# Decoder trunk on one core: weight sums beside the first three feed-forward out-projections, and the last residual loaded in four pieces

## The chip, the cores and the metric

One core of one Trainium2 chip runs the whole program. The metric is the device time of one execution in microseconds (us); lower is better. Before the change it is 2209.56 us, the median of 3 runs (2207.72 to 2211.31).

## The reference, cut to what matters

```python
D_MODEL = 1024; SEQ = 512; DEPTH = 2; D_FF = 2816

def _swiglu(x, w_in, w_out):
    gate, up = jnp.split(x @ w_in, 2, axis=-1)
    return (jax.nn.silu(gate) * up) @ w_out

for i in range(DEPTH):
    ng = norm_gains[i]
    x = x + 0.5 * _rmsnorm(_swiglu(_rmsnorm(x, ng[0]), ffn1_w_in[i], ffn1_w_out[i]), ng[1])
    h = _rmsnorm(x, ng[2])
    m = _hgrn2(h, ...) if i == 0 else _gated_deltanet(h, ...)
    x = x + _rmsnorm(m, ng[3])
    x = x + 0.5 * _rmsnorm(_swiglu(_rmsnorm(x, ng[4]), ffn2_w_in[i], ffn2_w_out[i]), ng[5])
```

All in float32, 512 tokens of 1024 features. The change touches no formula; it concerns the four feed-forward sub-layers, above all the last line of the second layer, `ffn2_w_out[1]`, and the last addition to `x`.

## The kernel before, in words

**Six stages**, numbered by `s`: feed-forward (0), HGRN2 (1), feed-forward (2 and 3), DeltaNet (4), feed-forward (5). `ffn_no` numbers the feed-forward stages 0 to 3. A float32 product is made of three TensorE passes over operands split in a high and a low part (high by high, high by low, low by high). Weights come as *units* of 128 x 1024 (512 KB) or, in the out-projections, 128 x 768 and 128 x 640. Each unit goes through a ring of four places: SP loads it into `raw`, ScalarE copies it to `w_hi` (L898, L972, in the last out-projection L1147 in `out_high`), VectorE subtracts and writes `w_lo` (L1679, L1798, L2013 in `out_low`), TensorE uses it. SP loads unit n when VectorE has split unit n - 4; ScalarE copies unit n when TensorE has used unit n - 4.

**A feed-forward stage** has an in-projection of some 230 us (six pairs of columns done plainly, L2830, the rest with seven products in place of eight, L2909) and then the out-projection, 8 tiles of 22 blocks of 128 rows each. In stages 0, 2 and 3 the tiles are ordinary ones: ScalarE squares each tile from PSUM into one of the two halves of `sq` (L1230), POOL adds the squares of tiles 0 to 6 up in `acc` (`total` in `sum8`, L2637 for the first and L2640 for the others), and TensorE reads `acc` in the middle of the last tile (L2820, `sum_outputs`). ScalarE's square of tile c waits for the sum of tile c - 2.

**The last out-projection** (stage 5, `out_products`) works by token tile, with seven products p = 0 to 6 of half-size matrices in place of eight. Each product takes 11 half units (128 x 512) of weights, so there are 77 half units, in 39 units n = 0 to 38. Products 0, 1 and 4 take their weights from `last_out` as they are. Products 2, 3, 5 and 6 take sums and differences of its four quarters. Those are not computed by an engine: POOL's queue makes them beforehand with accumulating DMA transfers in DRAM, into `w_sums`, 11 row tiles k of 128 x 4 x 512. Each k takes five transfers: 768 KB and 256 KB of plain copies, an add of 768 KB, an add of 768 KB, an add of 256 KB, where each add waits on `sums_added` until what went before it has landed. `weight_sums` does k = 0 to 5 in stage 2 and k = 6 to 10 in stage 3, each time before that stage's `sum8`, one k after the other. SP waits for all of them once, before unit n = 11.

**The order of the work in the last out-projection** is written out by hand. VectorE's loop calls `out_low(n)` for n = 4 to 38 and does other work after some of them: `part_low("s1")` after n = 15, `part_low("s4")` after n = 16 (L2007, the low parts of activation quarters), two `joined` after n = 20 (L2038), `part_low("s3")` after n = 21, `part_low("a22")` after n = 22. ScalarE's loop calls `out_high(n)`, and after n = 20 makes two high parts (`part_high`, L1140). SP's loop loads unit n (L812, two transfers of 256 KB), and after n = 20 it loads the residual by token, `x_tok` (2 MB, one transfer, L817), and the last gain row broadcast to 128 partitions into `out_gain` (512 KB, L818). `out_gain` lies in the memory of `y`, which the SwiGLU products of the last quad still read (`last_rows`, L1867, semaphore value `last_early`). VectorE waits for both transfers (`tok_loaded`) after its last `out_low`; then come the scalings L2047 and the final additions L2050.

Of the kernel before, what the change touches and what calls it, by code (L numbers as in the profile page):

```python
# [17 lines left out]
P = 128  # L18
TOK = 512
D = 1024  # L20
KD = D // P
# [17 lines left out]
KH = KF // 2  # L39
# [13 lines left out]
def trunk(nc, A, out, kinds=("ffn", "hg", "ffn", "ffn", "gd", "ffn")):  # L53
# [4 lines left out]
    ALU = mybir.AluOpType  # L58
# [3 lines left out]
    first_unit, total = [], 0  # L62
# [3 lines left out]
    ffn_no = {s: n for n, s in enumerate(s for s, k in enumerate(kinds) if k == "ffn")}  # L66
    LAST = len(kinds)

    ctx = ExitStack()
    with ctx:  # L70
# [140 lines left out]
        unit_used = sem("unit_used")  # L211
# [11 lines left out]
        x_rows_stored = sem("x_rows_stored")  # L223
        tok_loaded = sem("tok_loaded")
# [10 lines left out]
        act_ready = sem("act_ready")  # L235
# [4 lines left out]
        dve_rows = sem("dve_rows")  # L240
# [32 lines left out]
        sums_added = sem("sums_added")  # L273
# [217 lines left out]
        def last_early(s, t):  # L491
            return up_early(s, QUADS - 1, t) + 2
# [10 lines left out]
        def part_ready(name):  # L503
            return KF * (len(ffn_no) - 1) + PARTS.index(name) + 1
# [17 lines left out]
        def mixed(n):  # L522
            return DVE_ROWS * len(ffn_no) + n
# [200 lines left out]
        def _(sp):  # L724
# [15 lines left out]
            def ffn(s):  # L740
                u0 = first_unit[s]
                w_in = A["ffn_in"]
                w_out = A["ffn_out"]
                row0 = ffn_no[s] * 2 * KF

                def weights(row):
                    return w_in[row:row + 1, :, :].rearrange("a p n -> (a p) n")

                def rows_of(q):
                    return row0 + 2 * PLAIN + 8 * q  # L750

                def gate_quarter(q, a):
                    sp.wait_ge(joint_made, joint(s, q - 1, "rest", a))
                    sp.wait_ge(lo_split, unit_of(s, q - 1, 6) + a + 1 + SKEW)
                    sp.dma_start(gate_place(s, q, a), weights(rows_of(q) + a)).then_inc(quarter_loaded[0][a], 16)

                def lower_gate_quarter(q, a):
                    if q == 1:
                        sp.wait_ge(unit_used, u0 + 2 * PLAIN)
                    else:  # L760
                        sp.wait_ge(lo_split, unit_of(s, q - 2, 3) + a + 1 + SKEW)
                    sp.dma_start(lower_gate_place(s, q, a), weights(rows_of(q) + 2 + a)).then_inc(quarter_loaded[1][a], 16)

                def up_quarter(q, a):
                    if q == 0:
                        sp.wait_ge(unit_used, u0 + 2 * PLAIN)
                    else:
                        sp.wait_ge(lo_split, unit_of(s, q - 1, 7) + a + 1 + SKEW)
                    sp.dma_start(up_place(a), weights(rows_of(q) + 4 + a)).then_inc(quarter_loaded[2][a], 16)

                def lower_up_quarter(q, a):
                    if q == 0:
                        sp.wait_ge(unit_used, u0 + 2 * PLAIN)
                    else:
                        sp.wait_ge(lo_split, unit_of(s, q - 1, 4) + a + 1 + SKEW)
                    sp.dma_start(lower_up_place(s, q, a), weights(rows_of(q) + 6 + a)).then_inc(quarter_loaded[3][a], 16)

                for n in range(0 if s else RING, 2 * PLAIN):
                    load((u0 + n, 0), weights(row0 + n))
                if s == LAST - 1:  # L780
                    for c in range(KD):
                        sp.wait_ge(turned, c + 1)
                        for a in range(P // SUB):
                            src = x_turned[a * SUB:(a + 1) * SUB, :, :].rearrange("i c (b j) -> i c b j", j=SUB)
                            dst = x_rows.rearrange("(b i) (c a j) -> a i c b j", i=SUB, a=P // SUB, j=SUB)[a]
                            sp.dma_start(dst[:, c], src[:, c]).then_inc(x_rows_stored, 16)
                for n in range(2 * PLAIN, N_PLAIN):
                    load((u0 + n, 0), weights(row0 + n))
                for q in range(QUADS):
                    if q:  # L790
                        for a in range(2):
                            gate_quarter(q, a)
                        for a in range(2):
                            lower_gate_quarter(q, a)
                    for a in range(2):
                        up_quarter(q, a)
                        if q == 0:
                            lower_up_quarter(q, a)
                    if q:
                        for a in range(2):  # L800
                            lower_up_quarter(q, a)
                if s < LAST - 1:
                    out_loads(s, w_out, ffn_no[s] * KD)
                    return
                v0 = u0 + IN_UNITS["ffn"]
                for n in range(OUT_PARTS):
                    sp.wait_ge(lo_split, v0 + n - RING + 1 + SKEW)
                    if n == KH:
                        sp.wait_ge(sums_added, SUMS)
                    for a in range(half_weights(n) // TOK):  # L810
                        cols = slice(a * TOK, (a + 1) * TOK)
                        sp.dma_start(raw[:, (v0 + n) % RING, cols], half_source(2 * n + a)).then_inc(raw_loaded[(v0 + n) % RING], 16)  # L812
                    if n == 20:
                        sp.wait_ge(act_ready, part_ready("s1"))
                        sp.wait_ge(dve_rows, mixed(6))
                        sp.wait_ge(x_rows_stored, 16 * 4 * KD)
                        sp.dma_start(x_tok[:], x_rows.rearrange("(t p) d -> p t d", p=P)).then_inc(tok_loaded, 16)  # L817
                        sp.dma_start(out_gain, A["last_gain"].to_broadcast([P, D])).then_inc(tok_loaded, 16)  # L818

            def out_loads(s, w_out, row0):  # L820
                cuts = CUTS[kinds[s]]
# [852 lines left out]
        def _(dve):  # L1674
# [341 lines left out]
            def out_products(s):  # L2016
# [40 lines left out]
                for n in range(4, OUT_PARTS):  # L2057
# [38 lines left out]
                    elif n == 36:  # L2096
# [2 lines left out]
                            joined(5, i, right(2 + i), right(2 + i))  # L2099
                        for i in range(2):  # L2100
                            joined(5, i, left(2 + i), left(2 + i))
                dve.wait_ge(tok_loaded, 2 * 16)
                for t in range(2):
                    dve.wait_ge(tok_root, 3 + t)
                    gained(left(t), left(t), 1.0, 0)
# [525 lines left out]
        def _(pool):  # L2631
            def total(q, c, par, first=False):

                pool.wait_ge(sq_done, SQUARES * (q // 2) + KD * (q % 2) + c + 1)
                if first:
                    wait(pool, sum_ready, pre_sums(q // 2) if q else 0)
                    nc.gpsimd.tensor_copy(acc[:], sq[:, par, :]).then_inc(acc_done, 1)  # L2637
                else:
                    pool.wait_ge(acc_done, POOLED * q + c)
                    nc.gpsimd.tensor_tensor(acc[:], acc[:], sq[:, par, :], ALU.add).then_inc(acc_done, 1)  # L2640
# [122 lines left out]
                    if n == 3:  # L2763
                        substitute(range(23, SUB - 1))

            def weight_sums(ks):
                w = A["last_out"]

                def quarter(r, c, k, copies):
                    src = w[(r * KH + k) * P:(r * KH + k + 1) * P, c * TOK:(c + 1) * TOK]  # L2770
                    return src.unsqueeze(1).to_broadcast([P, copies, TOK])

                for k in ks:
                    n = 5 * 16 * k
                    sums = w_sums[k]
                    nc.gpsimd.dma_start(sums[:, 0:3, :], quarter(0, 0, k, 3)).then_inc(sums_added, 16)
                    nc.gpsimd.dma_start(sums[:, 3:4, :], quarter(0, 1, k, 1)).then_inc(sums_added, 16)
                    pool.wait_ge(sums_added, n + 32)
                    nc.gpsimd.dma_start(sums[:, 0:3, :], quarter(0, 1, k, 3), accum_op=ALU.add).then_inc(sums_added, 16)
                    pool.wait_ge(sums_added, n + 48)  # L2780
                    nc.gpsimd.dma_start(sums[:, 1:4, :], quarter(1, 1, k, 3), accum_op=ALU.add).then_inc(sums_added, 16)
                    pool.wait_ge(sums_added, n + 64)
                    nc.gpsimd.dma_start(sums[:, 2:3, :], quarter(1, 0, k, 1), accum_op=ALU.add).then_inc(sums_added, 16)
                    pool.wait_ge(sums_added, n + 80)

            nc.gpsimd.memset(ident[:], 0.0).then_inc(ident_made, 1)
            nc.gpsimd.memset(upper[:], 1.0).then_inc(ident_made, 1)
# [5 lines left out]
            for s, kind in enumerate(kinds):  # L2793
                if s == 0:
                    sum8(0)
                if kind != "ffn":
                    {"hg": hgrn2, "gd": deltanet}[kind](s)
                elif ffn_no[s] in (1, 2):
                    weight_sums(range(6) if ffn_no[s] == 1 else range(6, KH))
                if s < LAST - 1:  # L2800
                    sum8(2 * s + 1)

# [835 lines left out]
```

## Time and profile before

| | |
|---|---|
| median of 3 runs | 2209.56 us (2207.72 to 2211.31) |
| the profiled execution, its own time | 2208.14 us |
| its span | 2206.4 us |
| TensorE matmul busy | 2176.8 us, 99% |
| VectorE, ScalarE, POOL busy | 1598.8, 1164.8, 256.5 us |
| granted TensorE clock | full, but for the last us |
| DMA | 248.96 MB, of it 31.72 MB on POOL's software queue |

The profiled execution's own time is 1.7 us above its span and 1.4 us under the median. Matmul ends are modelled, so the idle time of weight loads (PEld) is the better measure of a short stop of TensorE: one load follows the other in 0.227 us when nothing waits.

### The profile page before, as it was taken

Reading aid. Unit: us, or ns where it says so; the run is one execution under the profiler, and the core shown is the slowest. Engines: PE = TensorE matmul, PEld = TensorE weight load, DVE = VectorE, ACT = ScalarE, POOL = GpSimd, SP = SyncE. Lnnn points to the kernel's source line nnn. Section 1 sums busy time; section 2 is a strip of 40 time slices with the busy share of each in tenths; the row PEclk is TensorE's granted clock in tenths of the full one; section 3 lists DMA queues with packets and bytes.
Section 4 is the critical chain, followed back from the end, with each engine's and each line's share of the span. In section 5 each row is a group of like instructions: output and inputs, shape, how many; then the busy total and the mean of one; then the engine's idle time right before and its main releaser. Section 6 shows DMA issues by size and latency. Waiting matters only on the chain.

```text
span 2206.4 us, 30954 instructions
## 1 busy us (share of the span) xinstructions
PE 2176.8 (99%) x11576; PEld 1804.4 (82%) x11576; DVE 1598.8 (72%) x2044; ACT 1164.8 (53%) x1648; POOL 256.5 (12%) x262
## 2 busy tenths in 40 slices
PE   9999999999999999999999999999999999999998
PEld 8888888888788888888788887777888888788876
DVE  6999536777568987348989337877766644898987
ACT  5455434655554455345445335577666744444563
POOL 2000000100121110011100000022822100000000
PEclk9999999999999999999999999999999999999999
DMA  5322332222267872367762332321212232433264
GB/s 173 125 86 81 108 98 87 87 76 78 69 155 182 225 160 86 97 151 167 192 180 66 99 102 67 101 77 55 83 56 68 68 95 78 116 134 124 86 219 157
DMA packets 106239, 248.96 MB, mean 113 GB/s; under 512 B 26848, under 2 KB 31072, under 8 KB 106112
## 3 DMA queue, kind: packets, MB, share of 16 engines
q1 hardware_dynamic: 92032, 215.24, 30.8%
q0 software_dynamic: 13552, 31.72, 8.1%
q8 instruction: 84, 1.38, 0.3%
q14 instruction: 43, 0.35, 0.1%
q10 hardware_dynamic: 528, 0.26, 0.0%
HBM read 242.93 MB, written 35.98 MB: 126 GB/s over the span
## 4 chain that ended last, share of the span: by engine, by line
PE 84%; DVE 10%; ACT 3%; DMA 1%; issue 1%; SPq 0%; DVEq 0%; ACTq 0%
PE bank L2830 38%; PE bank L2909 24%; PE bank L3275 9%; PE bank L3031 3%; DVE w_lo L1679 2%; PE bank L2983 1%; DVE h_lo L1684 1%; DVE w_lo L1798 1%; DMA raw_last<-in_ffn_in 1%; ACT h_hi L910 1%; ACT w_hi L898 1%; PE bank L3437 1%; DVE resid L1714 1%; PE bank L3416 1%; PE bank L3444 1%
## 5 line engine op out<-in xcount | busy, mean ns | idle before, releaser
L1679 DVE TENSOR_TENSOR w_lo<-raw,w_hi 128x1024 fp32r<-128x1024 f32 x261 | 321.1, 1242 | 334.5 <-ACT w_hi L898 334.1
L2909 PE MATMUL bank<-w_hi,factor 128*128 128x512 f32 x1792 | 553.8, 390 | 3.9 <-DVE w_lo L1798 3.7
L2909 PEld LDWEIGHTS bank<-w_hi,factor 128*128 128x128 f32 x1792 | 335.0, 188 | 75.2 <-issue 4.9
L898 ACT ACTIVATE w_hi<-raw 128x1024 fp32r<-128x1024 f32 x261 | 271.5, 1054 | 214.6 <-PE bank L2830 193.6
L2909 PE MATMUL bank<-w_lo,factor 128*128 128x512 f32 x896 | 349.1, 390 | 0.0
L2830 PE MATMUL bank<-h_hi,w_hi 128*128 128x512 f32 (+1 forms) x775 | 295.2, 381 | 5.7 <-DVE h_lo L1684 2.7
L2830 PE MATMUL bank<-h_hi,w_lo 128*128 128x512 f32 (+1 forms) x775 | 284.8, 367 | 0.0
L2830 PE MATMUL bank<-h_lo,w_hi 128*128 128x512 f32 (+1 forms) x748 | 274.6, 367 | 0.0
L2830 PE MATMUL bank<-act_late,w_hi 128*128 128x512 f32 (+1 forms) x648 | 200.7, 367 | 0.0
L2909 PEld LDWEIGHTS bank<-w_lo,factor 128*128 128x128 f32 x896 | 168.2, 188 | 35.2
L2830 PEld LDWEIGHTS bank<-h_hi,w_hi 128*128 128x128 f32 x775 | 146.2, 189 | 37.1 <-issue 6.5
L2830 PE MATMUL bank<-act_lo,w_hi 128*128 128x512 f32 (+1 forms) x540 | 169.6, 366 | 0.0
L2830 PEld LDWEIGHTS bank<-h_hi,w_lo 128*128 128x128 f32 x775 | 146.1, 189 | 24.5
L2830 PEld LDWEIGHTS bank<-h_lo,w_hi 128*128 128x128 f32 x748 | 141.2, 189 | 24.4 <-issue 2.6
L2830 PE MATMUL bank<-act_late,w_lo 128*128 128x512 f32 (+1 forms) x432 | 158.1, 366 | 0.0
L3275 PE MATMUL bank<-h_hi,w_hi 128*128 128x512 f32 x360 | 149.7, 416 | 1.2 <-DVE conv_in L2266 0.7
L3275 PE MATMUL bank<-h_hi,w_lo 128*128 128x512 f32 x360 | 148.4, 412 | 0.0
L3275 PE MATMUL bank<-h_lo,w_hi 128*128 128x512 f32 x360 | 147.3, 409 | 0.0
L2830 PEld LDWEIGHTS bank<-act_late,w_hi 128*128 128x128 f32 x648 | 118.8, 189 | 19.6
L972 ACT ACTIVATE w_hi<-raw_more 128x1024 fp32r<-128x1024 f32 x80 | 84.6, 1061 | 80.4 <-DVE raw_more L1814 32.7
L972 ACT ACTIVATE w_hi<-raw 128x1024 fp32r<-128x1024 f32 x72 | 76.4, 1061 | 70.3 <-PE bank L2909 56.8
L2830 PEld LDWEIGHTS bank<-act_lo,w_hi 128*128 128x128 f32 x540 | 99.5, 189 | 16.6
(388 smaller groups left out, 3959.0 us busy)
## 6 DMA issues: line engine op xcount, KB each, us to landing
raw<-in_ffn_in SPq DMA_DIRECT2D x84, 512.0 KB, 4.7
w_sums<-in_last_out POOLq DMA_DIRECT2D x33, 768.0 KB, 8.5
raw<-in_gd_in SPq DMA_DIRECT2D x49, 512.0 KB, 3.7
raw_more<-in_ffn_in SPq DMA_DIRECT2D x48, 512.0 KB, 4.8
raw_last<-in_ffn_in SPq DMA_DIRECT2D x40, 512.0 KB, 6.1
raw<-in_ffn_out SPq DMA_DIRECT2D x48, 384.0 KB, 3.1
raw<-in_hg_in SPq DMA_DIRECT2D x32, 512.0 KB, 3.7
raw<-in_ffn_out SPq DMA_DIRECT2D x48, 320.0 KB, 2.9
```

Source lines behind the costliest of these rows:

```text
L898: nc.scalar.activation(w_hi[:, u[0] % RING, :], raw[:, u[0] % RING, :], ACT.Copy).then_inc(hi_split, 1)
L910: nc.scalar.activation(h_hi[:, c, half(h)], x[:, c, half(h)], ACT.Copy, scale=pre_gain(s, c)).then_inc(h_hi_ready, 1)
L972: nc.scalar.activation(w_hi[:, u % RING, :], place, ACT.Copy).then_inc(hi_split, 1)
L1679: nc.vector.tensor_tensor(w_lo[:, r, :], raw[:, r, :], w_hi[:, r, :].bitcast(f32), ALU.subtract).then_inc(lo_split, 1)
L1684: nc.vector.scalar_tensor_tensor(out=h_lo[:, c, half(h)], in0=x[:, c, half(h)], scalar=pre_gain(s, c), in1=h_hi[:, c, half(h)].bitcast(f32 ...
L1714: nc.vector.tensor_tensor(x[:, c, half(h)], x[:, c, half(h)], y[:, i % 2, half(h)], ALU.add).then_inc(x_ready, 1)
L1798: TT(w_lo[:, u % RING, :], place, w_hi[:, u % RING, :].bitcast(f32), ALU.subtract).then_inc(lo_split, 1)
L2830: ins = nc.tensor.matmul(dst[:, half(h)], w, moving[ml][:, k, :][:, half(h)], start=first and n == 0 and (wl, ml) == (0, 0), stop=last and ...
L2909: ins = nc.tensor.matmul(bank[dst[t]][:], factor[:, 2 * i + ml, at:at + P], (w_hi, w_lo)[wl][:, u % RING, b * TOK:(b + 1) * TOK], start=st ...
L2983: ins = nc.tensor.transpose(dst[:, t * P:(t + 1) * P], rows[:, f * P:(f + 1) * P], ident[:])
L3031: ins = nc.tensor.matmul(product_bank(p, i)[:], operands[p][ml][:, k, i * P:(i + 1) * P], (w_hi, w_lo)[wl][:, u % RING, cols], start=k == ...
L3275: ins = MM(bank[unit_bank(n)][:], (w_hi, w_lo)[wl][:, (u0 + n) % RING, k * P:(k + 1) * P], (h_hi, h_lo)[ml][:, k, :], start=x == 0, stop=x ...
```

## The change

POOL's five transfers per k are no longer done k by k. In the out-projection of each of stages 0, 2 and 3, two groups of tiles k, `(0, 1), (2, 3)`, then `(4, 5), (6, 7)`, then `(8, 9), (10,)`, go through their steps between the seven `total` calls, the k's of a group together. The wait for a step's transfers stands after the next `total` and before the next step's transfers. `out_gain` is loaded after unit n = 5 instead of n = 20, behind a wait for unit 0's use and for `last_rows`. `x_tok` is loaded in four transfers of one token tile (512 KB) after units 20, 23, 26 and 29.

```diff
@@ sync, ffn, last out-projection
-                    if n == 20:
-                        sp.wait_ge(act_ready, part_ready("s1"))
-                        sp.wait_ge(dve_rows, mixed(6))
-                        sp.wait_ge(x_rows_stored, 16 * 4 * KD)
-                        sp.dma_start(x_tok[:], x_rows.rearrange("(t p) d -> p t d", p=P)).then_inc(tok_loaded, 16)
+                    if n == 5:
+                        sp.wait_ge(unit_used, v0 + 1)
+                        sp.wait_ge(dve_rows, last_early(s, 1))
                         sp.dma_start(out_gain, A["last_gain"].to_broadcast([P, D])).then_inc(tok_loaded, 16)
+                    if n in (20, 23, 26, 29):
+                        t = (n - 20) // 3
+                        if t == 0:
+                            sp.wait_ge(act_ready, part_ready("s1"))
+                            sp.wait_ge(dve_rows, mixed(6))
+                            sp.wait_ge(x_rows_stored, 16 * 4 * KD)
+                        sp.dma_start(x_tok[:, t, :], x_rows[t * P:(t + 1) * P, :]).then_inc(tok_loaded, 16)
@@ vector, out_products
-                dve.wait_ge(tok_loaded, 2 * 16)
+                dve.wait_ge(tok_loaded, 5 * 16)
@@ gpsimd
-            def weight_sums(ks):
...
+            SUM_TILES = (((0, 1), (2, 3)), ((4, 5), (6, 7)), ((8, 9), (10,)))
...
+            def begin_sums(ks):
                 for k in ks:
...
+                    nc.gpsimd.dma_start(w_sums[k][:, 0:3, :], quarter(0, 0, k, 3)).then_inc(sums_added, 16)
+                    nc.gpsimd.dma_start(w_sums[k][:, 3:4, :], quarter(0, 1, k, 1)).then_inc(sums_added, 16)
+
+            def add_to_sums(ks, added, a, b, r, c):
+                pool.wait_ge(sums_added, 16 * added)
+                for k in ks:
+                    nc.gpsimd.dma_start(w_sums[k][:, a:b, :], quarter(r, c, k, b - a), accum_op=ALU.add).then_inc(sums_added, 16)
+
+            def sum8_beside_sums(q, first, second):
+                n = 5 * first[0]
+                m = 5 * second[0]
+                f, g = len(first), len(second)
+                total(q, 0, 0, True)
+                begin_sums(first)
+                total(q, 1, 1)
+                add_to_sums(first, n + 2 * f, 0, 3, 0, 1)
+                total(q, 2, 0)
+                add_to_sums(first, n + 3 * f, 1, 4, 1, 1)
+                total(q, 3, 1)
+                add_to_sums(first, n + 4 * f, 2, 3, 1, 0)
+                begin_sums(second)
+                total(q, 4, 0)
+                add_to_sums(second, m + 2 * g, 0, 3, 0, 1)
+                total(q, 5, 1)
+                add_to_sums(second, m + 3 * g, 1, 4, 1, 1)
+                total(q, 6, 0)
+                add_to_sums(second, m + 4 * g, 2, 3, 1, 0)
@@ gpsimd, loop over the stages
-                elif ffn_no[s] in (1, 2):
-                    weight_sums(range(6) if ffn_no[s] == 1 else range(6, KH))
-                if s < LAST - 1:
+                if kind == "ffn" and s < LAST - 1:
+                    sum8_beside_sums(2 * s + 1, *SUM_TILES[ffn_no[s]])
+                elif s < LAST - 1:
                     sum8(2 * s + 1)
```

## Rows read from the trace of the kernel before

**Rows 1.** The page, busy time of each engine in the whole span.

```profile
PE 2176.8 (99%) x11576; PEld 1804.4 (82%) x11576; DVE 1598.8 (72%) x2044; ACT 1164.8 (53%) x1648; POOL 256.5 (12%) x262
```

**Rows 2.** Waits of weight loads, 2120 to 2165 us: us in total, times, longest.

```profile
PEld bank L3031 <- DVE w_lo L2013: 4.7, 4, 1.5
```

**Rows 3.** SP's queue from 2130 us: start, us, what was issued.

```profile
2133.03 0.37 SPq L817 DMA_DIRECT2D x_tok<-x_rows  x1
2136.26 0.82 SPq L812 DMA_DIRECT2D raw<-w_sums  x2
```

**Rows 4.** DMA, 2120 to 2165 us: count, KB each, median us to landing.

```profile
x_tok<-x_rows SPq DMA_DIRECT2D x1, 2048.0 KB, 8.8
y<-in_last_gain SPq DMA_DIRECT2D x1, 512.0 KB, 10.8
```

**Rows 5.** ScalarE from 2133 us: start, us, what ran, idle before, releaser.

```profile
2133.40 1.06 ACT L1147 ACTIVATE w_hi<-raw 128x1024 fp32r<-128x1024 f32 x1 [1.65 <-PE bank L3031]
...
2137.63 4.99 ACT L1140 ACTIVATE act_parts<-y_all 128x2816 fp32r<-128x2816 f32 x2
2145.72 1.06 ACT L1147 ACTIVATE w_hi<-raw 128x1024 fp32r<-128x1024 f32 x1 [3.11 <-DMA raw<-w_sums]
```

**Rows 6.** VectorE from 2135 us.

```profile
2135.01 4.62 DVE L2013 TENSOR_TENSOR w_lo<-raw,w_hi 128x1024 fp32r<-128x1024 f32 x4
...
2146.82 1.23 DVE L2013 TENSOR_TENSOR w_lo<-raw,w_hi 128x1024 fp32r<-128x1024 f32 x1 [5.98 <-ACT w_hi L1147]
2147.96 3.08 DVE L2007 TENSOR_TENSOR act_lo<-y_all,act_parts 128x2816 fp32r<-128x2816 f32 x1
2150.96 1.22 DVE L2013 TENSOR_TENSOR w_lo<-raw,w_hi 128x1024 fp32r<-128x1024 f32 x1
2152.09 3.08 DVE L2007 TENSOR_TENSOR act_lo<-y_all,act_parts 128x2816 fp32r<-128x2816 f32 x1
```

**Rows 7.** TensorE's weight loads at the first of those four stops.

```profile
2136.29 0.30 PEld L3031 LDWEIGHTS bank<-w_hi,act_parts 128*128 128x128 f32 x2 [0.63 <-DVE w_lo L2013]
```

**Rows 8.** Waits of weight loads in stage 3's in-projection, 980 to 1225 us.

```profile
PEld bank L2909 <- issue: 1.7, 2, 1.1
PEld bank L2909 <- DVE w_lo L1798: 1.4, 1, 1.4
```

**Rows 9.** The same waits in stage 2's in-projection, 630 to 870 us.

```profile
PEld bank L2909 <- issue: 1.1, 1, 1.1
...
PEld bank L2909 <- DVE w_lo L1798: 0.2, 1, 0.2
```

**Rows 10.** VectorE shortly before stage 3's longest stop.

```profile
1056.94 1.23 DVE L1802 TENSOR_TENSOR raw<-raw_more,raw 128x1024 f32<-128x1024 f32 x1 [1.18 <-DMA raw_more<-in_ffn_in]
```

**Rows 11.** VectorE at the start of the last out-projection.

```profile
2090.18 1.28 DVE L1867 TENSOR_TENSOR y_first<-y_first,y 128x512 f32<-128x512 f32 x2
...
2104.12 3.49 DVE L2013 TENSOR_TENSOR w_lo<-raw,w_hi 128x1024 fp32r<-128x1024 f32 x3
```

**Rows 12.** ScalarE's copy of unit 6 there.

```profile
2098.42 1.04 ACT L1147 ACTIVATE w_hi<-raw 128x1024 fp32r<-128x1024 f32 x1
```

**Rows 13.** POOL in stage 0's out-projection: first and last of its seven sums.

```profile
250.80 0.61 POOL L2637 COPY acc<-sq 128x512 f32<-128x512 f32 x1 [231.64 <-ACT sq L1230]
...
340.49 1.30 POOL L2640 TENSOR_TENSOR acc<-acc,sq 128x512 f32<-128x512 f32 x1 [13.50 <-ACT sq L1230]
```

**Rows 14.** TensorE's first reading of POOL's sum in stage 0.

```profile
350.41 0.60 PE L2820 MATMUL bank<-acc,ones 128*128 128x256 f32 x2
```

**Rows 15.** POOL's queue, the third step of the weight sums of k = 0.

```profile
641.41 1.26 POOL L2781 DMA_DIRECT2D w_sums<-in_last_out  x1 [10.62 <-DMA w_sums<-in_last_out]
```

**Rows 16.** DMA, 620 to 1140 us: packets, MB, share of 16 engines; one issue.

```profile
q0 software_dynamic: 13552, 31.72, 34.4%
...
raw_last<-in_ffn_in SPq DMA_DIRECT2D x18, 512.0 KB, 7.0
```

**Rows 17.** Stage 2's out-projection: five engines' busy time, clock, DMA share, GB/s.

```profile
880.00:970.00 90.00, 90.00 (x431) 75.94 (x431) 29.42 (x24) 31.29 (x36) 9.07 (x8) 1.00 0.39 109
```

More of the change, by code:

```diff
@@ L2764, in deltanet @@
                         substitute(range(23, SUB - 1))
-            def weight_sums(ks):
[L2767 to L2771, printed above, removed]
-                for k in ks:
[L2774 to L2784, printed above, removed]
@@ new lines, in _, with quarter @@
+            SUM_TILES = (((0, 1), (2, 3)), ((4, 5), (6, 7)), ((8, 9), (10,)))
+            def quarter(r, c, k, copies):
+                src = A["last_out"][(r * KH + k) * P:(r * KH + k + 1) * P, c * TOK:(c + 1) * TOK]
+                return src.unsqueeze(1).to_broadcast([P, copies, TOK])
+            def begin_sums(ks):
+                for k in ks:
+                    nc.gpsimd.dma_start(w_sums[k][:, 0:3, :], quarter(0, 0, k, 3)).then_inc(sums_added, 16)
+                    nc.gpsimd.dma_start(w_sums[k][:, 3:4, :], quarter(0, 1, k, 1)).then_inc(sums_added, 16)
```

## The prediction

> **What bounds the kernel now.** I read the page's busy times first: TensorE's matmuls are busy for 99% of the span [rows 1], so only what stops TensorE can cost or give time. Next I read the waits of its weight loads, stretch by stretch. Two stops have to do with the transfers that the change moves.
>
> The larger is in the last out-projection: 4.7 us in four stops, all for VectorE's `out_low` [rows 2]. Such an idle time holds 0.04 us of ordinary gap (a load of 0.19 us every 0.227 us), and after a stop two loads take 0.30 us where they otherwise take 0.42, so 0.12 us is caught up [rows 7]. Net loss: 4.7 - 4 x 0.16 = 4.1 us. The queue tells why. At 2133.03 SP issues 2 MB of residual and then 512 KB of gain, and only at 2136.26 unit 21 [rows 3]. The 2.5 MB land 8.8 and 10.8 us after issue [rows 4]. ScalarE ends its two high parts at 2137.63 + 4.99 = 2142.6 and then waits 3.1 us for unit 21 [rows 5], VectorE waits 5.98 us for ScalarE, and behind unit 21 it must do two low parts of 3.08 us, with unit 22 between them [rows 6]. So the lateness of unit 21 hits units 21, 22 and 23.
>
> The smaller is in stage 3's in-projection: 1.7 + 1.4 = 3.1 us of idle loads [rows 8] against 1.1 + 0.2 = 1.3 us at the same place of stage 2 [rows 9]. VectorE had waited 1.18 us for a weight unit there [rows 10], while the weight sums ran. Less 0.12 us caught up at its stop, and some 0.1 for the shorter one, about 1.6 us is lost. Stage 2 ran with such sums too and lost nothing more: it is a matter of phase.
>
> **The residual in four pieces, the gain early.** I work the queue out anew. Before unit 21 stand 512 KB in place of 2.5 MB. At the rate of the 2.5 MB (issued at 2133.0, the last landed at 2133.4 + 10.8 = 2144.2: 0.23 MB/us [rows 3, 4]) that is 2.3 us, so unit 21 lands by about 2141, before ScalarE is free at 2142.6. ScalarE then copies it to 2143.6. VectorE splits it from 2143.6 and goes on at its own pace (1.14 us to the next operation after a split, 3.0 after a low part [rows 6]): s3 from 2144.8, unit 22 from 2147.8 to 2149.0, a22 from 2148.9, unit 23 from 2151.9 to 2153.1. TensorE's times: a unit takes 12 x 0.227 = 2.72 us (ScalarE's 1.06 + 1.65 beside it [rows 5]); unit 17 starts at 2136.29 [rows 7], so 21 at 2147.2, 22 at 2149.9, 23 at 2152.6. Unit 21 is ready 2.4 us early, 22 by 0.9, 23 is 0.5 late. The first stop, 0.63 us, stays: unit 17 is the first of four splits that start at 2135.01 [rows 6], behind the low parts of s1 and s4, before any residual was asked for. Left are 0.63 - 0.16 = 0.5 and 0.5 - 0.1 = 0.4 us. **Gain: 4.1 - 0.9 = 3.2 us.** If TensorE had still to wait for the pieces, the gain would be less; its ends are 0 (unit 21 as late as now) and 4.1 (no stop left). I take 3.2, which follows from rows at 1 us from the place.
>
> The later pieces go after units 23, 26 and 29. Each puts 512 KB before the next unit, in a stretch where three units (1.5 MB) are used in 8.2 us. 2 MB in 8.2 us is 0.24 MB/us, about what the 2.5 MB and its followers got. The last is issued when unit 25 is split, near 2156, and is wanted after unit 38, some 30 us later. I cost them at nothing; the cover is the ring, which asks for a unit four units (10.9 us) before TensorE needs its place.
>
> The trace says nothing against small transfers there. The Trainium skill, DMA: Bandwidth & Descriptors, Measured, says the opposite of this edit: transfers should be 1 MiB or more, and each has a fixed cost of about 2 us. By that, three more transfers cost an estimated 6 us of DMA time, which would lie in the queue, not on TensorE, while units land in time. No row here shows 512 KB pieces of the residual.
>
> The gain row: SP now stops after unit 5 until `last_rows` ends at 2090.18 + 1.28 = 2091.5 [rows 11]. Queued behind it is unit 6, which now is asked for when unit 2 is split, some 2 us before that, and from then on with 512 KB ahead of it. ScalarE copies unit 6 at 2098.42 [rows 12], VectorE splits it at 2104.12 [rows 11]. Bounds: with the 7.0 us of a unit beside other traffic [rows 16] it lands near 2099 and is copied by 2100; with the 10.8 us of the loaded queue [rows 4] it lands at 2102.8 and is copied by 2103.9, still before VectorE's turn. Both ends are zero for TensorE. On the other side the change takes 512 KB out of the busy stretch (in the sum above).
>
> **The weight sums.** Removed from the in-projections: all their traffic. The extra stop of stage 3 goes, **1.6 us** (ends 0 and 1.8). Added to the out-projections of stages 0, 2 and 3: POOL's issues (22 + 33 as before, about 1 us each) and waits. Queued behind the waits is the next `total`; ScalarE waits for it a whole tile later, and TensorE for the last one. The seven sums are 14.96 us apart, from 250.80 to 340.49 [rows 13], and TensorE reads the result at 350.41 [rows 14]. The last `total` stands behind five waits (begin, two adds, the mixed step, an add). From 251.4 on, the fifth may end at 350.4 - 1.3 (sum) - 2.5 (two issues) = 346.6: **19.0 us per step** is the point from which TensorE waits. What is a step with two k's? One add of 768 KB took 1.3 + 10.6 = 11.9 us with its issue [rows 15]; two are 13.2 us if they overlap and 23.8 if not. POOL's queue used 34.4% of 520 us for 11 k's, 16.3 us of all sixteen engines per k [rows 16], so two k's need 32.5 us over four steps, 8.1 us each, more in the adds (about 11); the weights of the out-projection take 39% of the engines [rows 17]. 11 / 0.7 + 1.3 gives about 17 us; the mixed step 19, the first 16. Sum 16 + 3 x 17 + 19 = 86: TensorE's sum is ready some 9 us before its time. So zero, with ends at zero and at 5 x 23.8 - 95 = 24 us in each of two stages, some 12 in the third with its smaller second group.
>
> Weight units beside them: a load is asked for four units (15 us) before ScalarE's copy, and under the sums' traffic a 512 KB unit landed in 7.0 us [rows 16]. TensorE has three units more. Zero.
>
> **Sum.** 3.2 + 1.6 = 4.8 us off the profiled execution: 2208.1 to 2203.3. That execution is 1.4 us under the median of the three, so the median is predicted at 2209.6 - 4.8 = **2204.8 us**. About 0.2%, 4.4 us, is what a measurement of this kernel can tell from no change, so the forecast stands just beyond it.
>
> **Rivals.**
> 1. *Both stops go* (forecast), range 2203 to 2206. For: the queue's order and the times above. Chance 0.50.
> 2. *Only a part is real*: the stop of stage 3 is a matter of phase and may be missing in other executions or return elsewhere, or the pieces (a small transfer's fixed cost) keep unit 21 late by 1 to 2 us more. Gain 3.2 alone, or 1.6 + 1.5: 2206.4. Chance 0.28. Against: unit 21 has 1.5 us to spare before ScalarE.
> 3. *More goes*: no stop is left in the last out-projection, and stage 3 gives its upper end: 4.1 + 1.8 and up to 1 us elsewhere: 2203.2. Chance 0.12.
> 4. *POOL's last sum comes late* (slower). Place: the wait before the last `total`, then L2820. It decides above 19.0 us per step and outweighs the gain above 19.5. At 20 us a step it is 5 us late in stages 0 and 2: 2209.6 + 10 - 4.8 = 2214.8. For: the ends reach to 23.8. Against: the engine time. Chance 0.10, half of it beyond 0.2% slower. In a sentence that the sum does not need: the Trainium skill, DMA: Bandwidth & Descriptors, Arbitration, says each engine takes turns between queue rows packet by packet; POOL's adds would then get at least half of each engine beside SP's loads, 11 / 0.5 + 1.3 = 23 us a step at worst, and only while SP's row is never empty, which the 39% speaks against.
>
> **The numbers.** Faster by over 0.2%: 0.38 of case 1, 0.11 of case 3, a little of 2: 0.50. Slower: 0.06. Same: 0.44. The range 2202.0 to 2208.8 holds cases 1 to 3 and the spread of the medians; case 4 is left out.
>
> **What would show it.** Right: idle of weight loads at L3031 falls from 4.7 to about 1.2 us in two stops (units 17 and 23), unit 21 is not waited for by ScalarE; stage 3's in-projection idles like stage 2's; POOL's L2640 in stage 0 still starts near every 15 us and L2820 is never waited for. Wrong: a wait of L2820 for POOL, DMA waits of L1147 after 2142 us, or a stop of unit 6 near 2106.

## The result, and the profile after

The changed kernel is slower: 2230.81 us, the median of 4 runs (2230.01 to 2235.4), against 2210.43 us before (4 runs). The ratio is 1.0099, 95% interval 1.0084 to 1.0114, a loss of about 20 us. I had forecast 2204.8 us and a gain. The place where it was lost stood among the rivals as the fourth, with a chance of 0.10 and a price that was too small.

The profiled execution of the changed kernel is its slowest, 2235.4 us, with a span of 2233.6; the one before had 2206.4, so 27.2 us are to be explained there. (The change adds lines: L1140 is now L1145, L1147 is L1152, L1230 is L1235, L1679 is L1684, L2013 is L2018, L2640 is L2645, L2776 and L2777 are L2779 and L2780, all adds of the weight sums are L2785, L2820 is L2841, L2909 is L2930, L3031 is L3052.)

The waits of TensorE's weight loads in the whole span (us in total, times, longest):

```profile
PEld bank L2841 <- POOL acc L2645: 28.2, 2, 15.0
```

This line did not exist before. TensorE, in the middle of the last tile of an out-projection, twice waited for POOL's last sum of squares. POOL's queue in stage 0's out-projection shows the way there, from the first sum to the last transfer (compare [rows 13, 14]):

```profile
250.96 0.61 POOL L2642 COPY acc<-sq 128x512 f32<-128x512 f32 x1 [231.60 <-ACT sq L1235]
...
265.94 1.29 POOL L2645 TENSOR_TENSOR acc<-acc,sq 128x512 f32<-128x512 f32 x1 [11.64 <-ACT sq L1235]
267.19 1.32 POOL L2785 DMA_DIRECT2D w_sums<-in_last_out  x1
277.57 1.26 POOL L2785 DMA_DIRECT2D w_sums<-in_last_out  x1 [9.06 <-issue]
...
286.80 1.25 POOL L2785 DMA_DIRECT2D w_sums<-in_last_out  x1 [4.60 <-DMA w_sums<-in_last_out]
297.25 1.24 POOL L2785 DMA_DIRECT2D w_sums<-in_last_out  x1 [9.20 <-issue]
298.04 1.77 POOL L2645 TENSOR_TENSOR acc<-acc,sq 128x512 f32<-128x512 f32 x1
307.86 1.70 POOL L2785 DMA_DIRECT2D w_sums<-in_last_out  x2 [8.05 <-DMA w_sums<-in_last_out]
...
330.93 1.29 POOL L2785 DMA_DIRECT2D w_sums<-in_last_out  x1 [1.39 <-DMA w_sums<-in_last_out]
342.44 1.24 POOL L2785 DMA_DIRECT2D w_sums<-in_last_out  x1 [10.21 <-issue]
...
352.41 1.25 POOL L2785 DMA_DIRECT2D w_sums<-in_last_out  x1 [7.42 <-DMA w_sums<-in_last_out]
361.16 1.22 POOL L2785 DMA_DIRECT2D w_sums<-in_last_out  x1 [7.50 <-issue]
361.95 1.72 POOL L2645 TENSOR_TENSOR acc<-acc,sq 128x512 f32<-128x512 f32 x1
370.09 1.69 POOL L2785 DMA_DIRECT2D w_sums<-in_last_out  x2 [6.42 <-DMA w_sums<-in_last_out]
```

Two things are to be seen. The steps are longer than I took them: from one wait's end to the next 19.6, 21.1, 23.1 and 21.5 us. And the second transfer of a pair of adds is not issued after the first: POOL's queue stands still for 7.5 to 10.2 us with no semaphore to wait for ("issue"), and only then issues it. I call that a held issue. So the last sum, which stands behind a pair, starts at 361.95 in place of 340.49, and TensorE reads it at 363.7 instead of 350.4.

What the stop does to TensorE's clock, in the columns of [rows 17] (five engines' busy time, clock, DMA share, GB/s):

```profile
352.00:354.00 2.00, 0.00 (x0) 0.00 (x0) 0.00 (x0) 0.00 (x0) 1.25 (x1) 1.00 0.01 4
354.00:356.00 2.00, 0.00 (x0) 0.00 (x0) 0.00 (x0) 0.00 (x0) 0.00 (x0) 0.59 0.84 76
356.00:364.00 8.00, 0.28 (x1) 0.28 (x2) 0.00 (x0) 0.00 (x0) 2.51 (x2) 0.50 0.59 96
364.00:366.00 2.00, 2.00 (x6) 1.64 (x7) 0.00 (x0) 0.17 (x1) 0.00 (x0) 0.50 1.11 125
366.00:368.00 2.00, 2.00 (x12) 2.00 (x11) 0.91 (x2) 0.73 (x2) 0.00 (x0) 0.50 1.01 150
368.00:370.00 2.00, 2.00 (x18) 2.00 (x18) 0.61 (x1) 1.46 (x2) 0.00 (x0) 1.00 0.30 53
```

TensorE's last matmul before the stop ended at 350.7. The granted clock stays full until about 354.4 and is then at the lower of its two levels (1.2 GHz) until 368, 4.3 us after TensorE went on: 6 and 12 matmuls in 2 us, then 18. Stage 2's stop looks much the same, with 3.4 us at the lower level after it. The account of the profiled execution: 28.2 us of stops, less the 4.8 us that I had worked out for the two gains below, leaves 23.4; the span grew by 27.2. The 3.8 that remain are what 4.3 + 3.4 us at half clock cost, by this estimate.

The two gains that I had worked out are there. The waits of weight loads, first in the last out-projection (2130 to 2200 us), then in a stretch with stage 3's in-projection (980 to 1260 us):

```profile
PEld bank L3052 <- DVE w_lo L2018: 1.6, 2, 1.0
...
PEld bank L2930 <- issue: 1.1, 1, 1.1
```

That is 1.6 us in two stops where 4.7 in four stood [rows 2], and stage 3 idles as stage 2 did [rows 8, 9]. ScalarE no longer waits for unit 21 (compare [rows 5]):

```profile
2168.08 5.00 ACT L1145 ACTIVATE act_parts<-y_all 128x2816 fp32r<-128x2816 f32 x2
2172.98 1.04 ACT L1152 ACTIVATE w_hi<-raw 128x1024 fp32r<-128x1024 f32 x1
```

Behind unit 21, ScalarE does wait for the loads of units 22, 23 and 24, by 0.44, 0.29 and 1.48 us. I had called such waits a sign of being wrong. They cost nothing here: VectorE, which they could hold up, works without idle from 2174.05 us to past its split of unit 23 at 2182.33.

### The profile page after: what moved, and what is told of

Its sections match the earlier page's. It is cut to its first block, busy times and chain, and to the rows that moved or that the text cites. A ratio compares the mean times of both kernels' runs of the same rounds, so it can differ in the third digit from the quotient of the medians.

```text
span 2233.6 us, 30931 instructions
## 1 busy us (share of the span) xinstructions
PE 2179.4 (98%) x11576; PEld 1806.8 (81%) x11576; DVE 1599.9 (72%) x2044; ACT 1166.4 (52%) x1648; POOL 257.1 (12%) x262
## 4 chain that ended last, share of the span: by engine, by line
PE 75%; DVE 10%; issue 6%; DMA 3%; ACT 3%; POOL 1%; SPq 0%; DVEq 0%; ACTq 0%; POOLq 0%
PE bank L2851 30%; PE bank L2930 23%; PE bank L3296 9%; DMA w_sums<-in_last_out 3%; PE bank L3052 3%; DVE w_lo L1684 2%; PE bank L3004 1%; DVE h_lo L1689 1%; DVE w_lo L1803 1%; ACT h_hi L915 1%; POOL w_sums L2785 1%; ACT w_hi L903 1%; DVE resid L1719 1%; PE bank L3458 1%; PE bank L3437 1%
## 5 line engine op out<-in xcount | busy, mean ns | idle before, releaser
L1684 DVE TENSOR_TENSOR w_lo<-raw,w_hi 128x1024 fp32r<-128x1024 f32 x261 | 323.0, 1250 | 335.3 <-ACT w_hi L903 335.0
L2930 PE MATMUL bank<-w_hi,factor 128*128 128x512 f32 x1792 | 553.2, 390 | 2.8 <-DVE w_lo L1803 2.8
L2930 PEld LDWEIGHTS bank<-w_hi,factor 128*128 128x128 f32 x1792 | 335.0, 188 | 73.1 <-issue 4.3
L2930 PE MATMUL bank<-w_lo,factor 128*128 128x512 f32 x896 | 348.8, 389 | 0.0
L2930 PEld LDWEIGHTS bank<-w_lo,factor 128*128 128x128 f32 x896 | 168.2, 188 | 35.3
```

Of the source, the lines that this page charges most:

```text
L1684: nc.vector.tensor_tensor(w_lo[:, r, :], raw[:, r, :], w_hi[:, r, :].bitcast(f32), ALU.subtract).then_inc(lo_split, 1)
L2930: ins = nc.tensor.matmul(bank[dst[t]][:], factor[:, 2 * i + ml, at:at + P], (w_hi, w_lo)[wl][:, u % RING, b * TOK:(b + 1) * TOK], start=st ...
```

## The experiments

All were timed beside the kernel before: it took 2210.78 us (25 runs) beside e1 to e4, and 2210.24 us (25 runs) beside e5 to e8. Each ratio is to the kernel before, with its 95% interval.

**e1, SP's part alone.** The kernel before, with the diff of the SP queue and VectorE's wait; POOL as before.

> The kernel before with SP's part of the change alone (gain row after unit 5, residual in four pieces). Theory (the residual's part works as worked out, all of the loss comes from POOL): 3.2 us faster than before, idle of weight loads at the last out-projection 4.7 -> about 1.6 us in two stops, as in the changed kernel. Rival (part of the loss is here): same as before or slower.

2206.02 us; ratio 0.9982 (0.9973 to 0.9990), 4 us faster. The idle for `out_low` is 1.5 us in two stops. So this part does what was worked out, and none of the loss is here.

**e2, POOL's part alone.** The kernel before, with `sum8_beside_sums` in place of `weight_sums`; SP as before.

> The kernel before with POOL's part alone (weight sums in stages beside the out-projections). Theory (TensorE waits in stages 0 and 2 for POOL's last sum of squares): 20.4 + 3.2 = about 24 us slower than before, two waits of 12 to 15 us for POOL at the reading of the sum, none in stage 3, stage 3's in-projection idling like stage 2's. Rival (the two parts work on each other): anything under 18 us.

2235.89 us; ratio 1.0114 (1.0094 to 1.0134), 25 us slower. The waits of its weight loads (without SP's lines, L2841 is L2836 here, L3052 is L3047):

```profile
PEld bank L2836 <- POOL acc L2640: 26.5, 2, 13.6
PEld bank L3047 <- DVE w_lo L2013: 4.8, 4, 1.5
```

Two waits for POOL, and the four stops of before. The two parts add up: 25 less 4 is the 20 of the whole change, within the intervals.

**e3, more room for descriptors.**

```diff
-    nc = bacc.Bacc("TRN2", target_bir_lowering=False, num_devices=1, dynamic_dma_scratch_size=2048)
+    nc = bacc.Bacc("TRN2", target_bir_lowering=False, num_devices=1, dynamic_dma_scratch_size=3584)
```

2204.05 us; ratio 0.9971 (0.9962 to 0.9980). With this number alone the loss of 20 us becomes a gain of 6: it is worth some 26 us, and I had expected 20 to 25. POOL's queue from the first pair of adds on:

```profile
268.54 2.59 POOL L2785 DMA_DIRECT2D w_sums<-in_last_out  x2
282.26 1.30 POOL L2645 TENSOR_TENSOR acc<-acc,sq 128x512 f32<-128x512 f32 x1 [11.12 <-ACT sq L1235]
286.31 1.24 POOL L2785 DMA_DIRECT2D w_sums<-in_last_out  x1 [2.76 <-DMA w_sums<-in_last_out]
295.12 1.24 POOL L2785 DMA_DIRECT2D w_sums<-in_last_out  x1 [7.57 <-issue]
...
348.26 2.50 POOL L2785 DMA_DIRECT2D w_sums<-in_last_out  x2 [8.68 <-DMA w_sums<-in_last_out]
349.82 2.26 POOL L2645 TENSOR_TENSOR acc<-acc,sq 128x512 f32<-128x512 f32 x1
```

The first and the last pair are issued at once (2.59 and 2.50 us for two), pairs between are still held: POOL's idle put down to issue falls from 135 to 65 us, not under 50 as I expected. The first pair's step takes 17.8 us (268.54 to 286.31), and 19.6 in the changed kernel, where its second issue is held. The rival, that the engines' rate is all, falls. Counted from the first transfer, the last sum is ready 13.0 us earlier than in the changed kernel: 7.5 us because the last pair is issued at once, 5.5 us because the five steps are shorter (95.4 us in place of 100.9). It is just in time; TensorE waited 0.25 us for it.

**e4, the last total first.**

```diff
                 add_to_sums(second, m + 2 * g, 0, 3, 0, 1)
                 total(q, 5, 1)
+                total(q, 6, 0)
                 add_to_sums(second, m + 3 * g, 1, 4, 1, 1)
-                total(q, 6, 0)
                 add_to_sums(second, m + 4 * g, 2, 3, 1, 0)
```

> The changed kernel with the seventh total moved before the wait and the two adds that stood ahead of it; all transfers are as before. Theory (only that total's place behind the step costs time): it runs near 345 us of the span in stage 0, 5 us before TensorE reads the sum; no wait for POOL at either place, 4 to 5 us faster than the kernel before. Rival (what comes later on POOL's queue, the constants of stage 1 behind the last steps, or the transfers that run into the next stage, hold TensorE too): 0 to 10 us slower than before, with new waits after 357 us.

2203.35 us; ratio 0.9972 (0.9961 to 0.9982), 6 us faster than before and 27 faster than the changed kernel. The descriptors' room is the small one and the transfers wait as before; only one addition of 1.3 us stands elsewhere. POOL, and TensorE's reading of the sum:

```profile
342.04 1.24 POOL L2785 DMA_DIRECT2D w_sums<-in_last_out  x1 [11.05 <-issue]
342.83 3.21 POOL L2645 TENSOR_TENSOR acc<-acc,sq 128x512 f32<-128x512 f32 x2
351.90 1.25 POOL L2785 DMA_DIRECT2D w_sums<-in_last_out  x1 [5.86 <-DMA w_sums<-in_last_out]
```

```profile
350.21 0.31 PEld L2841 LDWEIGHTS bank<-acc,ones 128*128 128x128 f32 x2
```

The sum is ready at 346.0, 4 us before it is read. With e2 this settles the cause: the seventh `total` behind that pair of adds. The gain of 6 us is what the change is worth without it; I had worked out 4.8.

**e5, e3 and e4 together.**

> The changed kernel with the last total first (as in e4) and dynamic_dma_scratch_size 3584 (as in e3). Theory (each alone frees TensorE wholly, what they cure is one and the same wait): no further gain, within 1 us of e4, 2203 to 2204. Rival (POOL's late constants of stage 1, at 373 us in e4, still cost something): 1 to 3 us under e4.

2204.13 us; ratio 0.9975 (0.9964 to 0.9985). No further gain: both cure the same wait. POOL's constants of stage 1 come at 362 us here and at 373 in e4, so their lateness cost e4 nothing that these times show.

**e8, room between the two.** As e3, with 2816.

> The changed kernel with dynamic_dma_scratch_size 2816, between 2048 and 3584. Theory (room for descriptors): between the two, issue waits of POOL between 65 and 135 us, at least one of TensorE's two waits shorter than 13 us, time 2204 to 2225. Rival (3584 passes a threshold that 2816 does not): as the changed kernel, 2230.

2207.03 us; ratio 0.9988 (0.9979 to 0.9997). POOL's idle for issue is 53 us, below the 65 that I gave as the lower end and less than at 3584, yet TensorE still waits, 3.7 us in two waits. POOL's queue, and the first of the two waits:

```profile
268.06 2.60 POOL L2785 DMA_DIRECT2D w_sums<-in_last_out  x2
...
286.55 2.52 POOL L2785 DMA_DIRECT2D w_sums<-in_last_out  x2 [3.47 <-DMA w_sums<-in_last_out]
...
303.42 1.69 POOL L2785 DMA_DIRECT2D w_sums<-in_last_out  x2 [5.38 <-DMA w_sums<-in_last_out]
...
324.60 2.54 POOL L2785 DMA_DIRECT2D w_sums<-in_last_out  x2 [4.76 <-DMA w_sums<-in_last_out]
...
341.70 1.24 POOL L2785 DMA_DIRECT2D w_sums<-in_last_out  x1 [13.24 <-DMA w_sums<-in_last_out]
350.77 1.24 POOL L2785 DMA_DIRECT2D w_sums<-in_last_out  x1 [7.83 <-issue]
```

```profile
353.35 0.30 PEld L2841 LDWEIGHTS bank<-acc,ones 128*128 128x128 f32 x2 [1.94 <-POOL acc L2645]
```

**e6, the sums k by k in in-projections.** SP's part, `weight_sums` as before:

```diff
-                elif ffn_no[s] in (1, 2):
-                    weight_sums(range(6) if ffn_no[s] == 1 else range(6, KH))
+                elif ffn_no[s] in (0, 1):
+                    weight_sums(range(5) if ffn_no[s] == 0 else range(5, KH))
```

> SP's part of the change, and the weight sums k by k as in the kernel before, but k = 0 to 4 in stage 0 and 5 to 10 in stage 2, none in stage 3; each still before that stage's sum of squares. Theory (stage 3's longer stop came from the sums' traffic by its phase, stage 0 and 2 take six k's without loss): as e4, 2203 to 2205, 1.6 us under e1. Rival (the stop follows the sums to stage 0 or 2): as e1, 2206, with more idle of weight loads at L2914 in 20 to 250 us.

2209.92 us; ratio 0.9993 (0.9984 to 1.0002). My theory fell, and by more than the rival asked for. Waits of weight loads in stage 0's in-projection, then in stage 2's (in e6 and e1 L2909 is L2914, L1798 is L1803, L1802 is L1807):

```profile
PEld bank L2914 <- issue: 3.6, 2, 3.4
```

```profile
PEld bank L2914 <- issue: 3.7, 2, 2.6
...
PEld bank L2914 <- DVE w_lo L1803: 0.9, 1, 0.9
```

An undisturbed in-projection has 1.1 us in one. So 2.5 us are lost in stage 0 and 3.5 in stage 2, where the profile of before showed nothing extra. e1's profile has 3.9 us in stage 2 and nothing extra in stage 3. Its rows there show a late weight unit ahead of the stop, as [rows 10] did in stage 3:

```profile
705.03 1.23 DVE L1807 TENSOR_TENSOR raw<-raw_more,raw 128x1024 f32<-128x1024 f32 x1 [2.40 <-DMA raw_more<-in_ffn_in]
```

```profile
711.84 0.30 PEld L2914 LDWEIGHTS bank<-w_hi,factor 128*128 128x128 f32 x2 [3.68 <-issue]
```

So the stop goes where the sums go, and with one profile of each kernel its size differs from 0 to 3.5 us. That it changes from execution to execution of one kernel is not shown by a profile, but the times fit it: e1 lies between 2203.7 and 2210.2, the kernels that keep the sums out of the in-projections and free TensorE (e3, e4, e5, e7) all between 2201.9 and 2205.5.

**e7, VectorE's low parts later.** e4, and:

```diff
-                    elif n == 16:
+                    elif n == 18:
                         part_low("s4", ...)
-                    elif n == 21:
+                    elif n == 22:
                         part_low("s3", ...)
-                    elif n == 22:
+                    elif n == 26:
                         part_low("a22", ...)
```

> e4 with three of VectorE's low parts later in the last out-projection: s4 after unit 18 (was 16), s3 after 22 (was 21), a22 after 26 (was 22). Theory (the two stops that are left, at units 17 and 23, are VectorE's order and no transfer): both go, 0.9 us under e4, no idle of weight loads for out_low. Rival (unit 21 to 23 are still late for their transfers): the stop at 23 stays or moves.

2203.09 us; ratio 0.9968 (0.9956 to 0.9980). The stretch where the four stops stood:

```profile
2080.00:2160.00 80.00, 80.00 (x363) 66.50 (x362) 73.63 (x58) 48.12 (x45) 0.00 (x0) 1.00 0.69 225
```

TensorE is busy throughout and waits for no `out_low`, so both stops that were left were VectorE's order of work. In time it is 0.3 us under e4, not 0.9 as expected, with ranges that overlap: the trace shows the gain, the times do not resolve it. Its median is the lowest of all, by less than the spread.

## Why the prediction was wrong, point by point

- **The residual and the gain row** (predicted gain 3.2 us): right. e1 measured 4 us (interval 2.2 to 6.0); the two stops at units 17 and 23 were predicted at 0.63 and 0.5 us with the gap, and the changed kernel's profile has 0.64 and 1.00. Rows near the place, worked through engine by engine, carried this.
- **Stage 3's stop** (predicted 1.6 us): right in the profile, too small as a price. I took one execution's figure, and called stage 2's freedom from loss a fact; e6 and e1 show up to 3.5 us lost in an in-projection that holds the sums. e4 against e1 is 2.7 us by medians. The profile of before was a mild execution: 2208.14 us against a median of 2210.8 in 25 runs.
- **The step that failed** is the term "2.5 (two issues)": I let both transfers of a pair be issued in an issue's usual time twice. No row had two adds in flight, and I did not treat that as an operation not shown. At the decisive place the second issue was held for 7.5 us, so the two issues took 10.0 us in place of 2.5. The same hold broke the sum "16 + 3 x 17 + 19 = 86: TensorE's sum is ready some 9 us before its time". In its place stood 15.7 + 19.6 + 21.1 + 23.1 + 21.5 = 101 us (251.5 to 352.4). Where pairs went out at once, the forecast of a step held: 17.8 us for the first pair in e3, 16.9 to 18.5 in e8. With the mixed step at 21.2, in which an issue was still held, e8 came to 89.3 in all.
- **A slip in the sum.** The weights' loads took 39% of the engines by the row that I cited, which leaves 0.61, and I divided by 0.7, for which I gave no row. By 0.61 an add step is 11 / 0.61 + 1.3 = 19.3 us, the sum is at least 16 + 3 x 19.3 + 19 = 93 us, and some 2 us are to spare in place of 9; my own numbers did not carry a plain zero. That 17 came out near the 16.9 to 18.5 of the steps without a held issue is luck.
- **The point from which it decides** (19.0 us per step) was right. The measured mean of the five is 20.2, which gives 5 x 1.2 = 6 us, and the held issue 7.5 more: 13.5, against a wait of 13.2 us. Rival 4 named the place and the mechanism. It lacked the held issue, the clock after the stop, and so most of its price; 0.10 was too little for a term whose own bounds reached from 13.2 to 23.8 us around a threshold of 19.0.
- **The rule set beside it** (the Trainium skill, DMA: Bandwidth & Descriptors, Queues, rings and completion order, on arbitration) gave 23 us a step at worst. The changed kernel's steps of 19.6 to 23.1 us look like it, but they hold a held issue each, and the steps without one took 16.9 to 18.5. So no run here shows the adds held down to half of each engine.
- **The warning against transfers under 1 MiB** (the Trainium skill, DMA: Bandwidth & Descriptors, Measured) changed nothing that TensorE saw: e1 gained all that was worked out. The fixed cost of about 2 us, which I cited with it, stands elsewhere in the Trainium skill, DMA: Bandwidth & Descriptors, under Anatomy of one DMA — SWDGE (gpsimd) path, for transfers that POOL issues; the residual's are SP's.

## What to carry to other kernels

An in-order queue that issues transfers beside a computation puts every later operation behind the issue, too, and an issue is not free: ask how many transfers are in flight that never were together before. Put the operation that the critical engine reads ahead of the transfers, even when there seem to be 9 us to spare; e4 cost nothing and was worth 27 us. When a threshold lies between the bounds of an unmeasured step, the case beyond it is no small rival.

## What the runs showed of the hardware

With `dynamic_dma_scratch_size` at 2048, POOL's issue of the second accumulating 768 KB transfer of a pair was held for 7.4 to 10.7 us while the first was in flight. At 3584 and 2816 some pairs went out in 2.5 to 2.6 us, others were still held, for 7.6 to 9.8 us in stage 0. A pair of such adds in DRAM that went out at once took 16.9 to 18.5 us from its issue to the end of the wait for both (e3's first pair, e8's first three), in an out-projection whose weight loads took 35% of the DMA engines before the change (250 to 355 us). And in stops of 13.2 and 15.0 us TensorE's clock fell to 1.2 GHz some 4 to 5 us into the stop and came back 4.3 and 3.4 us after its end, which made each stop about 2 us dearer than its wait, by estimate.
